# Identity products of 128 columns into an unread bank, written ahead of six waits of TensorE

## What is computed

```python
# layer 0, mixer A: attention over a chunk and its 8 predecessors, 8 heads of 64, with a bias
s = einsum("bcqhd,bckhd->bchqk", qc, kb) * dh**-0.5 + bias ; p = softmax(s) ; o = einsum("bchqk,bckhd->bcqhd", p, vb)

# layer 1, mixer C: RWKV-7 recurrence (the kernel computes it in chunks of 64 tokens)
S = S * w_t + (S @ -kk_t) (x) (kk_t * a_t) + v_t (x) k_t ; y_t = S @ r_t

# layer 1, mixer D: latent attention, 8 heads, scores over 64 + 32 features, block-causal
s = (einsum("bqhd,bkhd->bhqk", qn, k_nope) + einsum("bqhd,bkd->bhqk", qp, k_pe)) * scale
p = softmax(where(key_chunk <= q_chunk, s, NEG_INF)) ; o = einsum("bhqk,bkhd->bqhd", p, v)
```

## Time and profile before

| | |
|---|---|
| median of three runs | 2412.57 us (2412.35 to 2412.82) |
| the profiled execution, its own time | 2411.99 us |
| its span, first to last instruction | 2409.9 us |
| mean granted TensorE clock | 0.977 |
| PE busy | 2271.8 us (94%) |
| DVE busy | 1167.2 us (48%) |
| ACT busy | 941.7 us (39%) |
| layer 0 attention in the trace | about 166 to 219 us |
| recurrence | about 797 to 1024 us |
| latent attention | about 1044 to 1094 us |

### The profile page before, as it was taken

How to read it: one execution, slowest core, us unless ns; L and a number is a source line. 1 busy time by engine, 2 the same in 40 slices (tenths; PEclk the granted TensorE clock), 3 DMA queues, 4 the chain that set the end, 5 groups by cost and what they waited for, 6 DMA issues and landing times.

```text
span 2409.9 us, 37786 instructions
## 1 busy us (share of the span) xinstructions
PE 2271.8 (94%) x15401; PEld 1936.1 (80%) x15401; DVE 1167.2 (48%) x1563; ACT 941.7 (39%) x1176; POOL 119.8 (5%) x177
## 2 busy tenths in 40 slices
PE   7988899999999888989899999999999998999995
PEld 6864888888878777648777787777779998999995
DVE  3267443323254678473588888888984000001001
ACT  4247332222242444273267767676763000000001
POOL 6101000000000000000000101010000000000000
PEclk9999999999999999999799999999999999999997
DMA  6320232242222000110699999999998768768663
GB/s 195 111 84 5 71 105 88 95 137 79 96 88 78 7 3 2 37 36 1 230 358 349 371 352 369 349 369 347 368 352 287 257 222 266 263 227 272 228 224 112
DMA packets 262116, 451.16 MB, mean 187 GB/s; under 512 B 8359, under 2 KB 148494, under 8 KB 261854
## 3 DMA queue, kind: packets, MB, share of 16 engines
q1 hardware_dynamic: 257216, 435.73, 51.7%
q0 software_dynamic: 4576, 13.41, 2.2%
q10 hardware_dynamic: 190, 0.05, 0.0%
HBM read 436.63 MB, written 12.52 MB: 186 GB/s over the span
## 4 chain that ended last, share of the span: by engine, by line
PE 86%; DVE 6%; ACT 5%; issue 2%; DMA 1%; ACTq 0%; DVEq 0%; POOLq 0%; SPq 0%; POOL 0%
PE bank L704 83%; PE bank L707 3%; DVE w_low L2056 1%; DVE arena L2056 1%; DVE slot L2056 1%; ACT w_high L1974 1%; ACT arena L1588 0%; ACT arena L1689 0%; ACT arena L1597 0%; DMA xs<-sum_rows_d 0%; ACT arena L1565 0%; DMA sum_rows_d<-arena,idx_now 0%; DMA vec_rows<-in_b_norm_w_dram 0%; DVE arena L2798 0%; ACT slot L1698 0%
## 5 line engine op out<-in xcount | busy, mean ns | idle before, releaser
L2056 DVE TENSOR_TENSOR w_low<-slot,w_high 128x2048 fp32r<-128x2048 f32 x172 | 393.7, 2292 | 324.0 <-ACT w_high L1533 257.4
L704 PE MATMUL bank<-arena 128*128 128x144 f32 (+6 forms) x2672 | 345.1, 299 | 7.3 <-DVE small L2215 2.5
L704 PEld LDWEIGHTS bank<-arena 128*128 128x128 f32 (+4 forms) x2672 | 312.3, 183 | 23.1 <-issue 11.2
L704 PE MATMUL bank<-arena,slot 128*128 128x144 f32 (+4 forms) x2368 | 313.0, 303 | 11.3 <-issue 6.7
L2056 DVE TENSOR_TENSOR arena<-arena,bank 128x512 f32<-128x512 f32 (+2 forms) x99 | 58.7, 593 | 529.8 <-PE bank L704 529.8
L704 PEld LDWEIGHTS bank<-arena,slot 128*128 128x128 f32 (+2 forms) x2368 | 289.7, 185 | 30.6 <-issue 23.9
L2056 DVE TENSOR_TENSOR w_low<-arena,w_high 128x2048 fp32r<-128x2048 f32 x105 | 240.0, 2290 | 25.9 <-ACT w_high L1974 25.1
L1974 ACT ACTIVATE w_high<-slot 128x2048 fp32r<-128x2048 f32 x108 | 206.2, 1915 | 71.5 <-PE bank L704 39.3
L704 PE MATMUL bank<-w_high,xg_high 128*128 128x512 f32 x560 | 227.2, 406 | 6.2 <-DVE w_low L2056 4.2
L1974 ACT ACTIVATE w_high<-arena 128x2048 fp32r<-128x2048 f32 x105 | 201.1, 1920 | 62.2 <-PE bank L704 62.2
L704 PE MATMUL bank<-h_ffn,w_high 128*128 128x512 f32 (+1 forms) x736 | 222.5, 385 | 0.8 <-DVE w_low L2056 0.8
(11 more groups left out here) (367 smaller groups left out, 3276.7 us busy)
## 6 DMA issues: line engine op xcount, KB each, us to landing
slot<-in_moe_w_up_dram SPq DMA_DIRECT2D x86, 1024.0 KB, 6.0
arena<-in_moe_w_gate_dram SPq DMA_DIRECT2D x78, 1024.0 KB, 6.2
arena<-in_moe_w_down_dram SPq DMA_DIRECT2D x64, 1024.0 KB, 5.1
slot<-in_moe_w_down_dram SPq DMA_DIRECT2D x48, 1024.0 KB, 5.4
slot<-in_moe_w_gate_dram SPq DMA_DIRECT2D x34, 1024.0 KB, 5.0
arena<-in_moe_w_up_dram SPq DMA_DIRECT2D x26, 1024.0 KB, 5.3
slot<-in_e_w_in_dram SPq DMA_DIRECT2D x12, 1024.0 KB, 6.0
slot<-in_ff_w_gate_dram SPq DMA_DIRECT2D x11, 1024.0 KB, 5.1
```

Of the source, the lines that this page charges most:

```text
L704: return pe.matmul(o, lhsT, rhs, start=start, stop=True, skip_group_check=True)
L2056: return dve.tensor_tensor(o, a, b, op)
```

## The change

A helper writes `n` products of the identity with itself, 128 columns wide, into a bank. It is called six times, always with `acc[0]`, which nobody reads before it is overwritten. The products wait for nothing and signal nothing. They add 96 products: 16 and 16 in the first attention, 24 and 16 in the recurrence, 12 and 12 in the latent attention.

```diff
+            def filler(n, b):
+                for i in range(n):
+                    mm(b[:, 0:P], ident[:, :], ident[:, :], True)
...
 # latent_attention
                 for p in range(HEADS // 2 * NT + 3):
+                    if p < 2:
+                        filler(12, acc[0])
...
 # attention of layer 0
                 for p in range(HEADS // 2 * NT + 3):
+                    if p in (1, 2):
+                        filler(16, acc[0])
...
 # recurrence
                 for t in range(NT):
+                    if t in (0, NT - 1):
+                        filler(24 if t == 0 else 16, acc[0])
                     for i, name in enumerate((f"al{t % 2}", "rt", "bt", "kt")):
                         pe.wait_ge(sem("scaled_ready"), 6 * t + i + 1)
```

## The result

| | median | runs | lowest to highest |
|---|---|---|---|
| before | 2412.32 us | 20 | 2410.25 to 2414.22 |
| with the 96 products | 2415.83 us | 20 | 2413.86 to 2418.58 |

The ratio is 1.0015, with a 95% interval of 1.0008 to 1.0022: the change costs 1.9 to 5.3 us, 3.5 at the medians. That is clear of noise, and smaller than the 0.2% (4.8 us) that the prediction named as its bound.

The account below looks back on a forecast made before the run. TensorE was taken to bound the kernel, with 86% of the span. The places' 2.4 + 0.0 + 3.2 + 4.8 = 10.4 us gave a forecast of 2423.0 us, slower by 0.43%, in a range of 2416 to 2428.

Parts of the forecast that it names:

- Price of a product: All blocks: one unread product takes 0.25 us at full clock, so the six blocks take 24.0 us in all.
- The rival of half a price: All blocks: a product costs 0.125 us, so blocks fit the waits; sum +0.2, 2412.8 us; chance 0.09.
- TensorE drops what nobody reads: Rival, all blocks: the unread products are dropped and the change does nothing; part of the last 5%.
- Layer 0: First attention, blocks of 16 and 16: maxima 3 come 2.4 us late, and the delay stays behind them.
- Tile 0: Recurrence, block of 24: the clock no longer falls and pays for the block in full, 0.0 us at the masks.
- Tile 3: Recurrence, block of 16: 4.0 us late for TensorE, less 0.8 of VectorE slack, so 3.2 us.
- Latent attention: Blocks of 12 and 12, 3.0 us each, partly hidden: 4.8 us later.
- The sum: Whole kernel: 2.4 + 0.0 + 3.2 + 4.8 = 10.4 us slower, 2423.0 us; chance 0.64.
- nothing behind the three places can take a delay back: Whole kernel behind the two attentions and the recurrence: a stage that starts late ends late.
- The clock beyond my sum: Four cold stretches, 13.0 us long, that the sum leaves as they are: together worth 3.9 us if the clock stayed up.
- the clock stays up behind the blocks as well: Rival: later cold stretches go too, 10.4 - 3.9 = 6.5 us slower, 2419.1 us, down to 2416.5; chance 0.14.
- Nothing of a block is hidden: Rival: blocks are hidden only in plain standstills of TensorE, 17.7 us slower, 2430.3 us; chance 0.08.

Follow-up runs that it names:

- e2: Kernel before plus only the two blocks of 16 products in the attention of layer 0: 2410.37 us, ratio 0.9990.
- e4: Kernel before plus only the block of 16 products ahead of tile 3 of the recurrence: 2411.40 us, ratio 0.9994.
- e1: Kernel before plus only the two blocks of 12 products in the latent attention: 2414.14 us, ratio 1.0007.
- e3: Kernel before plus only the block of 24 products ahead of tile 0 of the recurrence: 2408.52 us, ratio 0.9985.
- e5: Kernel before, no blocks, its 16 warm-up products of 384 columns written as 32 of 192 (64 more instructions): 2408.39 us, ratio 0.9989.
- e7: Kernel before, unchanged, run and traced a second time: 2411.35 us, ratio 1.0000.
- e8: Kernel before plus one block of 64 products ahead of scores 0 of the latent attention (256 more instructions): 2425.22 us, ratio 1.0056.
- e9: Kernel before plus only a block of 16 products ahead of tile 0 of the recurrence: 2407.62 us, ratio 0.9985.
- e10: Kernel before plus 8 products ahead of layer 0's scores 1, 8 ahead of its first transposes, 16 ahead of tile 0: 2404.86 us, ratio 0.9973.
- e6: Changed kernel with its 16 warm-up products of 384 columns written as 48 of 128 (512 more instructions than before): 2418.98 us, ratio 1.0032 to before.
- e11: As e10, plus 12 products inside tile 3 ahead of the transposes of the latent rows: 2402.18 us, ratio 0.9960 to the kernel before.

## Why the prediction was wrong

**Price of a product: right.** 0.25 was forecast and 0.236 measured at 166.65, 0.223 to 0.230 in the other places. The rival of half a price is refuted by the same rows, and so is the one that TensorE drops what nobody reads.

**Layer 0: right where it was worked out, not carried to the stage's end.** 2.4 was forecast at maxima 3 and 2.07 came. But the step let nothing move behind that, and at 200.2 the stage is only 0.9 late in the changed kernel and 0.0 in e2. The cold stretch from 180.7, which the step left as it is, did stay, but it covers other work: before it lay over eight transposes and over scores of 384 columns (1.65 against 0.92); after, those scores take 0.92 at 184.13. That stretch is one more thing that changes between executions: it is absent in e2, with the same two blocks, and in e4, with none. Traces with no block in the stage end it 0.3 to 1.9 us sooner than before's trace does, each against its own start. Where the stretch is missing, the blocks cost 1.9 us at the stage's end (e2 against e4), nearly the 2.07 of maxima 3; where it is there, 0.9 against before and 1.3 to 1.5 against the others of the same kind (e1, e3, e5, e7, e8). So most of the 2.07 may well be carried on, and how much stays open. The medians of e2 (+0.85 with the code's part taken out) agree with any of these.

**Tile 0: forecast 0.0, measured -0.7 against the trace before.** The block took 5.44 us (808.48 to 813.92) instead of 6.0, and from the transposes' start to the masks it was 3.47 instead of 3.58: 0.67 in all. The clock paid for the block, as forecast. But the other half of the comparison, the 10.42 us of before, was one of two values that an unfilled tile 0 has.

**Tile 3: forecast 3.2, measured 2.7,** with every trace with the block alike and 0.0 to 0.2 in those without. The block took 3.68 us (955.16 to 958.84) instead of 4.0, and VectorE's slack came out at 1.0, where the step said 0.8. The cold stretch behind it has grown to 6.6 us and lies over the 20 transposes (4.53 us), but the +1.1 of that row of the table isn't the block's: e5, with no block, has +1.0 there.

**Latent attention: forecast 4.8, measured 4.2.** The two blocks took 2.75 us (1048.84 to 1051.59) and 2.68 (1052.03 to 1054.71) instead of 3.0 each, and that is all of the difference.

**The sum: this step failed.** It has 10.4 us for the places of the change, where the trace shows 8.2 (2.1 - 0.8 + 2.7 + 4.2). Of the 6.9 us between the sum and the 3.5 of the medians that is 2.2, and size only. The larger part is a term that the sum did not have: **-2.75 us for what 384 more instructions do to the first turn of the narrow expert loop**. That nothing behind the three places can take a delay back holds (e8); work far behind changed for another reason. The two give 10.4 - 2.2 - 2.75 = 5.45 us, and the profiled execution was 5.16 later than the one before. That this agrees within 0.3 is partly luck: the 1.15 us that layer 0 seemed to lose behind maxima 3, and +0.8 of the stages with no block, are left out and nearly cancel. The medians differ by 3.5: that execution lay 1.3 above the median of its kernel, and the one before 0.3 below. The step also reckoned that runs of one kernel differ by up to 0.2 us, from three of them; the twenty runs of before span 4.0.

**The clock beyond my sum: its basis was wrong.** e5 and e7 run the same instructions as before up to the warm-up ahead of the experts. Growth of the shift by stage, from their timelines:

| stage, by before's time | e7 | e5 | after |
|---|---|---|---|
| 200.2 to 262.9 | 0.0 | +1.2 | +1.0 |
| 262.9 to 703.1 | 0.0 | +1.1 | +0.9 |
| 703.1 to 817.3 | 0.0 | -1.1 | -0.8 |
| 817.3 to 950.0 | 0.0 | -1.2 | -1.2 |
| 968.1 to 990.8 | 0.0 | +1.0 | +1.1 |
| 1047.2 to 1095.3 | 0.0 | +1.3 | -1.4 |

e7 repeats the trace before to the tenth. e5 differs from it by 1.0 to 1.3 us in six stages, with no edit in any of them, and the changed kernel moves the same way in five (in one of them, 703.1 to 817.3, it also has a block). So the clock can fall in these different ways in one and the same program, and the step's 3.9 us, priced from one trace, mixed them with what the blocks do. The rival "the clock stays up behind the blocks as well" gave 2419.1, and 2416.5 if each cold stretch gives back half. That was nearest to the measured 2415.83, but by luck: of the four stretches that it spoke of, the one at 180.7 stayed, the two in tile 3 became one as long as both, and the one at 1068.2 also goes where no block is near (e4, e9, e10).

By the rule of the Trainium skill in that step ("TensorE: Matmul & The Clock Gate", section "Terms") the stretch at 808.80 would be worth 3.3 us; at the masks e9 got back 1.0 to 2.0.

**Nothing of a block is hidden:** refuted. It asked for 17.7 us, and the price with the standstill as before (e6) is 7.7, 10.6 at most.

## What to carry to other kernels

Unread products in a standstill pay only as far as they end with the wait: ahead of tile 0, 16 in 3.8 us brought the masks 1.0 to 2.0 us nearer and 24 about nothing (the whole times don't tell the two apart), and 16 where there was no wait cost 2.7. Of the six places of the change only two, the first of layer 0 and tile 0, stood in a wait; look for the wait at the instruction that ends it, since it may lie one further on than the block. Before an effect of some 0.1 to 0.3% is put down to an edit, look far behind it for standstills without a releaser, and lengthen the code of the kernel before by instructions that add no work. Here 64 were enough; fewer were not tried, and by theory B a few would only move the cut by as many. And a stretch of low clock in one profile is not yet a property of the kernel: take a second profile of it before pricing one.

## What the runs showed of the hardware that was not expected

- **The length of TensorE's code decides about a standstill in a loop's first turn.** With 0, 256 and 512 more instructions TensorE stands still without a releaser for 1.48 to 1.84 us after 15 records of the narrow expert loop (before, e7, e8, e6); with 64, 96, 128, 176 or 384 it does not (nine kernels). In time that is 2.4 to 2.75 us in eight of the nine, since the clock also stays down longer, and 4.0 in e11. That the dependence is on the length is shown, for these eight lengths. That code comes in pieces of 256 instructions agrees with the fetch queue, 107 transfers of 16384 bytes, 108 with 256 more instructions and 109 with 512. One of them lands 1.2 to 1.5 us ahead of the end of the standstill; that TensorE waits for it is inferred. The standstill of 5.2 us ahead of it is in every trace, with a fetch inside it, and removing it was not tried.
- **A float32 product of 128 columns with the identity** takes 0.223 to 0.236 us at 2.4 GHz, two MATMUL records and four instructions.
- **The same instructions meet the falls of the clock differently in different executions,** by 1.0 to 1.3 us in each of six stages (e5 against e7).
